# A decoder layer with attention and mLSTM: who splits the second weights of each slot in the mLSTM heads

## What is computed

```python
h = rmsnorm(x, norm_w) * (1 + scale) + shift            # shift, scale, gate from silu(c) @ w_ada + b_ada
aq, ak, av, az, mq, mk, mv, mo, mz, mi, mf, ga, gm = split(h @ w_in)
att = sliding_window_attention(rope(aq), rope(ak), av, sinks)       # 16 heads, 4 of keys and values
y_att = (att * silu(az)) @ w_att
mq, mk = silu(causal_conv(mq, conv_q)), silu(causal_conv(mk, conv_k)) * 256 ** -0.5   # 4 taps
hm = mlstm_chunkwise(mq, mk, mv, i_pre, logf)                       # 4 heads of width 256
hm = rmsnorm_per_head(hm, m_norm_w) * sigmoid(mo)
y_m = (hm * silu(mz)) @ w_m
merged = sigmoid(ga) * y_att + sigmoid(gm) * y_m
out = rmsnorm(x + gate * (merged @ w_out), final_norm_w)
```

## Time and profile before

| what | value |
|---|---|
| median of three runs | 1438.28 us |
| profiled execution, span from first to last instruction | 1435.3 us |
| mean granted TensorE clock | 0.979 of full speed |
| TensorE busy | 1340.0 us, 93% of the span |
| VectorE busy | 750.4 us, 52% |
| GpSimd busy | 491.6 us, 34% |
| ScalarE busy | 396.6 us, 28% |
| splits on GpSimd, high part | 101 of 1994 ns mean |
| splits on GpSimd, low part | 101 of 2546 ns mean |

### The profile page before, as it was taken

The page is one execution under the profiler, slowest core; times in us unless marked ns, Lnnn a source line. Parts: engine busy times, 40 slices in busy tenths (PEclk is TensorE's granted clock), DMA queues, the critical chain, the costliest instruction groups (busy, mean ns, idle before and its releaser), DMA issues.

```text
span 1435.3 us, 19403 instructions
## 1 busy us (share of the span) xinstructions
PE 1340.0 (93%) x6846; PEld 1138.8 (79%) x6846; DVE 750.4 (52%) x1297; ACT 396.6 (28%) x926; POOL 491.6 (34%) x248
## 2 busy tenths in 40 slices
PE   2399998999989999999999999999999999899998
PEld 2297796978867888877988898889789888788886
DVE  5979888695776000065256426633672421366445
ACT  5342634334342010013221322233223311311111
POOL 4613204132045343273054205412531333335230
PEclk9599999999999999999999999999999999999999
DMA  9501102011021121050041004101310123322502
GB/s 350 137 15 30 45 2 59 15 29 29 0 58 35 54 88 59 15 162 16 1 117 44 0 0 132 29 0 41 91 44 15 44 74 98 107 76 68 193 16 103
DMA packets 119830, 89.28 MB, mean 62 GB/s; under 512 B 13305, under 2 KB 111721, under 8 KB 118894
## 3 DMA queue, kind: packets, MB, share of 16 engines
q1 hardware_dynamic: 116288, 76.16, 17.8%
q10 hardware_dynamic: 3502, 12.61, 2.5%
HBM read 80.35 MB, written 8.41 MB: 62 GB/s over the span
## 4 chain that ended last, share of the span: by engine, by line
PE 78%; DVE 14%; issue 4%; ACT 2%; DMA 1%; POOL 1%; DVEq 0%; ACTq 0%; SPq 0%; POOLq 0%
PE pp L527 22%; PE pp L529 22%; PE pp L528 22%; DVE conv L1382 2%; PE pp L713 2%; PE pp L723 2%; PE pp L633 1%; DVE prob L1232 1%; DVE y_lo L1289 1%; PE pp L624 1%; PE pp L602 1%; PE pp L616 1%; PE pp L705 1%; PE pp L617 1%; PE pp L718 1%
## 5 line engine op out<-in xcount | busy, mean ns | idle before, releaser
L482 POOL TENSOR_TENSOR w_hi<-raw,ones 128x1024 fp32r<-128x1024 f32 x101 | 201.4, 1994 | 828.6 <-ACTq L346 492.0
L527 PE MATMUL pp<-h_hi,w_hi 128*128 128x512 f32 x912 | 363.1, 398 | 14.8 <-DVE h_lo L1115 9.5
L528 PE MATMUL pp<-h_lo,w_hi 128*128 128x512 f32 x912 | 357.6, 392 | 0.0
L529 PE MATMUL pp<-h_hi,w_lo 128*128 128x512 f32 x912 | 357.1, 392 | 0.0
L484 POOL TENSOR_TENSOR w_lo<-raw,w_hi 128x1024 fp32r<-128x1024 f32 x101 | 257.2, 2546 | 7.9
L527 PEld LDWEIGHTS pp<-h_hi,w_hi 128*128 128x128 f32 x912 | 172.9, 190 | 52.6 <-issue 10.3
L529 PEld LDWEIGHTS pp<-h_hi,w_lo 128*128 128x128 f32 x912 | 172.6, 189 | 36.7
L528 PEld LDWEIGHTS pp<-h_lo,w_hi 128*128 128x128 f32 x912 | 172.9, 190 | 35.2
L527 PE MATMUL pp<-w_hi,h_hi 128*128 128x384 f32 (+1 forms) x512 | 162.1, 317 | 0.6 <-DVE roped L1209 0.6
L529 PE MATMUL pp<-w_hi,h_lo 128*128 128x384 f32 (+1 forms) x512 | 158.2, 309 | 0.0
L528 PE MATMUL pp<-w_lo,h_hi 128*128 128x384 f32 (+1 forms) x512 | 158.0, 309 | 0.0
(11 more groups left out here) (216 smaller groups left out, 1947.6 us busy)
## 6 DMA issues: line engine op xcount, KB each, us to landing
raw<-w_in SPq DMA_DIRECT2D x72, 512.0 KB, 3.8
w_mod<-w_ada SPq DMA_DIRECT2D x7, 1024.0 KB, 11.1
x_in<-x SPq DMA_DIRECT2D x4, 1024.0 KB, 8.2
raw<-w_att SPq DMA_DIRECT2D x8, 512.0 KB, 5.1
merged_dram<-mix_a ACTq DMA_DIRECT2D x8, 512.0 KB, 2.6
w_gate<-w_ada ACTq DMA_DIRECT2D x8, 512.0 KB, 3.5
raw<-w_m SPq DMA_DIRECT2D x8, 512.0 KB, 3.7
mix_in<-merged_dram ACTq DMA_DIRECT2D x8, 512.0 KB, 3.3
```

Of the source, the lines that this page charges most:

```text
L482: pool.tensor_tensor(hi, raw[:, s, :, :], one, ALU.mult).then_inc(slot_hi[s], 1)
L527: pe.matmul(o, lh, rh, start=first, stop=False)
L528: pe.matmul(o, lh, rl, start=False, stop=False)
L529: return pe.matmul(o, ll, rh, start=False, stop=last)
```

## The change

In phase C GpSimd splits only the first contents of each slot. The second contents' high part is made by ScalarE with a plain copy (`second_hi`), their low part by VectorE with the same subtraction as before (`second_lo`). For slots 0 to 3 ScalarE does it right after it has copied an odd unit of mq or mk into `xpad`, ahead of the SiLU, and VectorE right after the four taps. For slot 4 ScalarE does it behind the gate of unit mz1, and VectorE between its work for units mv1 and mv2. Nothing changes on TensorE and in the order of the DMAs; what SP waits for before it loads a slot again is now partly counted up by VectorE.

```diff
--- before.py
+++ after.py
@@ -501,7 +501,7 @@
                 for s in range(4):
                     split(s, use("B", s, 1) + i, loads("B", s, 2) + i)
             with pool.Fori(0, MH, 1) as i:
-                for n, (_, s, k) in enumerate(C_LOADS):
+                for n, (_, s, k) in enumerate(C_LOADS[0:5]):
                     split(s, use("C", s, k) + 2 * i, loads("C", s, k + 1) + 2 * i)
                     if n == C_MASK_AFTER - 1:
                         pool.wait_ge(dec_loaded, 16 * (i + 1))
@@ -910,6 +910,12 @@
                     act.dma_start(dst, mix_a[:, k:k + 1, :]).then_inc(mix_stored[k], 16)
 
 
+            def second_hi(i, s):
+
+                after(act, slot_free[s], use("C", s, 1) + 2 * i)
+                act.wait_ge(slot_loaded[s], 16 * (before(SLOT_DMAS, "C", s) + 2 + 2 * i))
+                act.activation(w_hi[:, s, :, :], raw[:, s, :, :], ACT.Copy).then_inc(slot_hi[s], 1)
+
             def conv_out(i, kind, n):
                 after(act, conv_step, 4 * (4 * i + n // 2 + (2 if kind == "mk" else 0) + 1))
                 act.activation((mk_t if kind == "mk" else mq_t)[:, n // 2, :], conv[:, :], ACT.Silu).then_inc(conv_silu, 1)
@@ -935,6 +941,8 @@
                             after(act, conv_step, 4 * (4 * i + f))
                             after(act, h_turned, 4 * i)
                         act.activation(xpad[:, CW - 1 + (n % 2) * HALF:CW - 1 + (n % 2 + 1) * HALF], bank(b), ACT.Copy).then_inc(bank_free[b], 1)
+                        if n % 2:
+                            second_hi(i, C_SLOT[f"{kind}{n // 2}"][0])
                         if n % 2 and (kind, n) != ("mk", 3):
                             conv_out(i, kind, n)
                     if kind == "mv":
@@ -957,6 +965,8 @@
                             conv_out(i, "mk", 3)
                             after(act, mask_added, i + 1)
                             decays(0, 2)
+                        if n == 1:
+                            second_hi(i, 4)
                     if kind == "mo":
                         after(act, gate_m_done, 4 * i + n)
                         act.activation(sig_o[:, :], bank(b), ACT.Sigmoid).then_inc(bank_free[b], 1)
@@ -1318,6 +1328,11 @@
             dve.wait_ge(cols_step, 3)
             dve.memset(v_aug[:, :, MD:MV], 1.0).then_inc(cols_step, 1)
 
+            def second_lo(i, s):
+
+                after(dve, slot_hi[s], use("C", s, 2) + 2 * i)
+                dve.tensor_tensor(w_lo[:, s, :, :], raw[:, s, :, :], w_hi[:, s, :, :].bitcast(F32), ALU.subtract).then_inc(slot_split[s], 1)
+
             def decay_scores(i, n):
                 after(dve, s_full, NB * i + n + 1)
                 after(dve, dec_ready, NB * i + n + 1)
@@ -1381,6 +1396,9 @@
                                 after(dve, conv_step, 4 * (4 * i + f) + j)
                                 dve.scalar_tensor_tensor(out=conv[:, :], in0=xpad[:, j:j + S], scalar=taps[:, j, n // 2:n // 2 + 1],
                                                          in1=conv[:, :], op0=ALU.mult, op1=ALU.add).then_inc(conv_step, 1)
+                        second_lo(i, C_SLOT[f"{kind}{n // 2}"][0])
+                    if (kind, n) == ("mz", 1):
+                        second_lo(i, 4)
                     if kind == "mv":
                         decay_scores(i, n)
                         if n >= 1:
```

## The result

The changed kernel took 1426.80 us (median of 4 runs, 1424.63 to 1429.24) beside 1438.26 us for the kernel before (4 runs, 1436.29 to 1438.99). The ratio is 0.9927, 95% interval 0.9913 to 0.9941: 11.5 us faster by the medians, where 8.0 had been forecast. A second series, of more runs, gave 1426.46 (5 runs) beside 1436.36 (21 runs), ratio 0.993, 0.9916 to 0.9943, or 9.9 us.

A forecast was written before the change was run, and what follows sets the result against it. TensorE, busy 93% of the span, was taken as the bound, its waits in the mLSTM heads as the gain: 6.8 + 1.2 = 8.0 us off the span 1435.3, so 1427.3, plus 3.0 gives 1430.3 us; range 1428.5 to 1433.5.

The forecast's parts named there:

- The collision and its place: Convolution of mk3: taps stand still while GpSimd splits slot 3; freed, it takes 4.8 us, at most 5.6, against 7.6.
- The rival of a convolution that stays slow: Something else beside VectorE slows the convolution; it stays 7.6 us, all five waits stay, time 1438.3; 7%.
- Four waits for `mk_t`, 6.8 us: TensorE's wait for mk_t, one a head, goes whole: 1.7 us a head, 6.8 us over four heads.
- Head 0, the second wait, 1.2 us: Head 0, second convolution: TensorE's second wait for xpad goes, worth between 1.00 and 1.39 us, taken as 1.2.
- The first wait stays: Head 0, first convolution: it lies beside first contents still split by GpSimd, so the 2.0 us wait for xpad stays.
- the slower matmuls behind it: Head 0: the slower TensorE matmuls after the first wait for xpad were to stay along with that wait.
- The third rival: Head 0's first wait goes too, some 2 us plus the slow matmuls after it: about 1426.5; 4%.
- ScalarE's five copies, VectorE's five subtractions, cost 0: Per head, copies at 1.23 us and subtractions at 1.22 us fit into idle time and delay TensorE nowhere: cost 0.
- a sign of being wrong: Listed signs: a ScalarE wait for raw<-w_in, slow taps without GpSimd, or new TensorE waits for state or v_aug.
- The slower rival: Head 0: ScalarE's copy for slot 0 waits for a late DMA; landing at 645 would give 1443; 4%.
- the worst case: Head 0, second convolution: VectorE's subtraction and first tap both wait for GpSimd's slot 4 split; three taps end at 642.2.
- The sum against the base: 8.0 us off the span 1435.3 gives 1427.3; the same 3.0 us from span to median 1438.28 gives 1430.3.

The follow-up runs named there:

- poolwait: Kernel before, all work left in place; GpSimd only waits for the convolution beside it before splitting second contents of slots 0 to 3: 1427.25 us, ratio 0.9935.
- slot3: Changed kernel with only slot 3's second contents split by ScalarE and VectorE, the other four left on GpSimd: 1429.85 us, ratio 0.9956 against the kernel before.
- not3: Changed kernel with second contents of slots 0, 1, 2 and 4 moved, slot 3 left on GpSimd: 1435.22 us, ratio 0.9987 against the kernel before.
- hionly: Changed kernel without second_lo: ScalarE makes the second contents' high part, GpSimd the low part behind it: 1432.57 us, ratio 0.9965 against the kernel before.
- mask5: Changed kernel with the mask's DMA and its addition on GpSimd behind slot 4's first contents instead of behind slot 1: 1422.10 us, ratio 0.9895 against the kernel before.

## Why the prediction was right or wrong

*The collision and its place.* This was right, and it is shown: the taps take 0.75 and, three together, 3.92 us without GpSimd, where the forecast had 0.81 and 3 x 1.30. `poolwait` isolates the collision, and `slot3` and `not3` put it at mk3. The rival of a convolution that stays slow is out. In `hionly` GpSimd comes second, and its 2.4 us become 3.5. The Trainium skill, "SBUF — State Buffer", section "Who interferes with whom", states that whoever comes second is blocked; by that rule, the trace agrees.

*Four waits for `mk_t`, 6.8 us.* Heads 1 to 3 measure 1.7 to 1.8 us each, so the 1.7 was right to 0.1 us a head. `slot3` alone brought 6.5 us.

*Head 0, the second wait, 1.2 us.* The mechanism was right, the size only for one case. With the clock down behind the first wait head 0 gains 2.9 us, which is the 1.7 and 1.2 of the forecast. With the clock up it gains 4.8, and in the mean of the four profiles 3.8: the term is 2.1 us there, not 1.2. The sum took one profile's wait of 1.00 us as the worth of removing it. In that profile TensorE was slow just ahead of it, which shortens a wait whose end another engine sets. The chain on VectorE's side (the end of the second convolution) was the bound of head 0 in either case; read as a bound, it would have shown that the price moves with TensorE's pace.

*The first wait stays.* This was right: 2.1 us are left. That "the slower matmuls behind it" stay too was wrong in two of four profiles. The third rival tied them to GpSimd leaving the first convolution; in fact they are there or not with the convolution unchanged. That rival's time, about 1426.5, is nearly the one measured, but by luck: its mechanism, the first wait gone, did not happen.

*ScalarE's five copies, VectorE's five subtractions, cost 0.* This was right. A copy takes 1.06 us (1.23 was taken), a free subtraction 1.22. ScalarE does wait for the DMA of slot 0 in head 0, which the prediction had named as a sign of being wrong. The wait comes early enough to cost nothing, 8 us before the SiLU behind it:

```profile
623.02 1.06 ACT L917 ACTIVATE w_hi<-raw 128x1024 fp32r<-128x1024 f32 x1 [2.43 <-DMA raw<-w_in]
...
631.26 1.06 ACT L921 ACTIVATE mq_t<-conv 128x1024 f32<-128x1024 f32 x1 [5.88 <-DVE conv L1397]
```

The slower rival had asked for a landing after 640. In head 0 the subtraction of slot 0 and the first tap behind it took 2.91 and 2.86 us beside GpSimd and took nothing from the gain: the second convolution ended at 640.8, where the worst case had 642.2. No wait of TensorE for `state` or `v_aug` appeared behind the fifth pair.

*What the list of waits left out.* The prediction placed all other long waits outside the heads. The list of the kernel before has one more row inside them, about as large as that of the two for `xpad`:

```profile
PE pp L752 <- DVE num L1399: 2.9, 6, 0.6
```

The change left these six waits as they were, so the sum did not suffer, but `mask5` won more there than at the first convolution.

*The sum against the base.* This is the step that put the time outside the range. The forecast took 8.0 from 1438.28, the median of three runs, and let the range reach only 1.8 us below the 1430.3. The first pair of profiles takes the 11.5 us apart. C gives 8.2 of them, beside 8.0 forecast. Before C lie 1.2 (615.7 to 614.5) and behind it 0.4, where the change touches nothing and profiles of one kernel differ by as much. Another 0.5 come from the changed kernel's profiled run, 1427.27, which lies above the median of its four. The last 1.2 are the base. The prediction carried the 3.0 us between its profile's span and its median over "with the same 3.0 us", but every run whose own span is on record takes only 1.7 to 1.9 us more than it. By that the profiled execution took about 1437.1 us (an estimate, 1435.3 and 1.8), and the rest of the 3.0 was the distance between that execution and three slower ones.

Later medians of the kernel before are 1436.4 (21 runs), 1436.5 (11) and 1437.7 (16), which is 0.6 to 1.9 us below that base. The spread of one kernel, 4.5 us, is more than half of the effect; "about 0.2%" was named as what a measurement can tell and not used for the range. So the forecast failed in two sizes, not in its mechanism. The base and the range around it left no room for the scatter, and head 0's second wait was priced at 1.2 us where the mean of four profiles gives 2.1 (C gains 9.1 where 8.0 was forecast). That the first pair of profiles shows 8.2 in C is in part luck: in both the clock fell in head 0.

## What to carry to other kernels

Look for instructions of one kind and size whose durations differ, and lay the other engines' timelines beside them: a wait of TensorE for ScalarE was here a GpSimd instruction two engines away, and holding GpSimd back was worth as much as moving its work. Price a wait that another engine's chain ends by that chain's end, not by the wait's length in one profile. And before a range is drawn around an effect of half a per cent, the base wants more runs than three, and the profiled execution has to be placed among them.

## What the runs showed of the hardware

After the same idle time of 2.0 to 2.3 us in the same place TensorE went on at 1.2 GHz for a while in five of eight profiles and at 2.4 GHz in three; in the four profiles of `slot3`, `not3`, `poolwait` and `hionly`, after 2.0 to 2.2 us, it was 1.2 GHz each time. Small instructions of VectorE can be hit harder in proportion than the taps beside GpSimd: in `mask5` eight copies of 128x2 took 6.9 us in place of 1.1. And moving a subtraction to VectorE made VectorE's busy time fall by 21 us, since the slowed taps had counted their standing still as work: the 64 taps took 128.6 us before and 81.6 after, the twenty subtractions 26.1.
